# Steps of an RWKV scan moved among the levels of a block inverse, and two exponentials split

## The reference, cut to what matters

```python
# decay, keys and rates, for each direction d (1 runs backwards)
w_raw = heads(w0[d] + jnp.tanh(xw @ w1[d]) @ w2[d])
decay = jnp.exp(-jnp.exp(-jax.nn.softplus(-w_raw) - 0.5))
a = jax.nn.sigmoid(heads(a0[d] + (xa @ a1[d]) @ a2[d]))
k_d = kh * (1 + (a - 1) * k_a_h)
...
def step(S, inp):
    w_t, k_t, v_t, kk_t, kka_t = inp[:5]
    S = (S * w_t[:, :, None, :]
         - jnp.einsum('bhij,bhj->bhi', S, kk_t)[..., None] * kka_t[:, :, None, :]
         + v_t[..., None] * k_t[:, :, None, :])
    y = jnp.einsum('bhij,bhj->bhi', S, inp[5]) if emit else None
    return S, y
```

## Time and profile before

| | us |
|---|---|
| median of 3 runs | 4827.68 (4825.2 to 4829.55) |
| the profiled execution | 4823.43 |
| its span, first to last instruction | 4821.6 |
| PE busy in the span | 4601.2 (95%) |
| DVE busy | 2700.9 (56%) |
| ACT busy | 1047.4 (22%) |
| the rounds of the scan, from 1434.9 to 2171.0 | 736.1 |

### The profile page before, as it was taken

The page is one execution under the profiler, slowest core; times in us unless marked ns, Lnnn a source line. Parts: engine busy times, 40 slices in busy tenths (PEclk is TensorE's granted clock), DMA queues, the critical chain, the costliest instruction groups (busy, mean ns, idle before and its releaser), DMA issues.

```text
span 4821.6 us, 70246 instructions
## 1 busy us (share of the span) xinstructions
PE 4601.2 (95%) x29914; PEld 3255.1 (68%) x29914; DVE 2700.9 (56%) x4820; ACT 1047.4 (22%) x2337; POOL 81.2 (2%) x81
## 2 busy tenths in 40 slices
PE   8999999998999899899999999989999999989998
PEld 5556555555546666665887788645887788645886
DVE  3172445535336776653555766674656766674656
ACT  1052100002016666642001110152001010151000
POOL 0000000000000000000000000020000000020000
PEclk9998999998999999998999999989999999989999
DMA  5211122221200000012222222211222122211221
GB/s 237 105 45 53 54 105 108 116 79 46 83 0 3 3 3 3 3 38 96 88 88 88 73 79 78 97 53 53 88 88 96 70 88 79 88 53 70 88 88 44
DMA packets 27046, 339.09 MB, mean 70 GB/s; under 512 B 3024, under 2 KB 3024, under 8 KB 6896
## 3 DMA queue, kind: packets, MB, share of 16 engines
q1 hardware_dynamic: 24048, 324.51, 17.9%
q0 software_dynamic: 2688, 10.09, 0.6%
HBM read 330.40 MB, written 4.19 MB: 69 GB/s over the span
## 4 chain that ended last, share of the span: by engine, by line
PE 88%; DVE 7%; ACT 4%; issue 2%; DMA 0%; SPq 0%; ACTq 0%; DVEq 0%
PE ps L1363 45%; PE ps L1081 23%; PE ps L1562 2%; PE ps L1153 2%; PE ps L1534 1%; PE ps L1493 1%; PE ps L1545 1%; PE ps L1610 1%; PE ps L1123 1%; ACT arena L1803 1%; PE ps L1304 1%; PE ps L1618 1%; PE ps L1431 1%; PE ps L1483 1%; DVE arena L2293 1%
## 5 line engine op out<-in xcount | busy, mean ns | idle before, releaser
L1363 PE MATMUL ps<-arena 128*128 128x256 f32 (+1 forms) x9096 | 2112.7, 395 | 15.1 <-DVE arena L2629 15.1
L1363 PEld LDWEIGHTS ps<-arena 128*128 128x128 f32 x9096 | 1735.9, 191 | 379.6 <-DVE arena L2629 17.5
L1081 PE MATMUL ps<-arena 128*128 128x512 f32 (+3 forms) x3104 | 1153.4, 533 | 10.7 <-ACT arena L1754 7.4
L1081 PEld LDWEIGHTS ps<-arena 128*128 128x128 f32 x3104 | 585.6, 192 | 566.4 <-issue 401.2
L2620 DVE TENSOR_TENSOR arena<-ps,arena 128x512 f32<-128x512 f32 (+1 forms) x250 | 157.6, 630 | 316.1 <-PE ps L1363 314.3
L2620 DVE TENSOR_TENSOR square<-ps,square 128x512 f32<-128x512 f32 (+1 forms) x145 | 99.1, 683 | 175.9 <-PE ps L1363 175.9
L2561 DVE TENSOR_TENSOR arena<-arena 128x1024 f32<-128x1024 f32 (+2 forms) x153 | 190.5, 1245 | 8.7 <-ACT arena L1754 5.4
L1944 ACT COPY square<-ps 128x512 f32<-128x512 f32 (+1 forms) x65 | 37.2, 573 | 659.3 <-PE ps L1363 591.9
L1562 PE MATMUL ps<-arena 64*64 64x64 f32 x3072 | 133.6, 230 | 19.9 <-ACT arena L2017 19.2
L2881 DVE COPY_PREDICATED arena<-const,ps 128x256 f32<-128x256 int32 x192 | 85.3, 445 | 114.2 <-PE ps L1562 111.0
L1944 ACT COPY arena<-ps 128x384 f32<-128x384 f32 (+1 forms) x35 | 18.5, 529 | 575.1 <-PE ps L1363 549.2
(11 more groups left out here) (341 smaller groups left out, 4868.4 us busy)
## 6 DMA issues: line engine op xcount, KB each, us to landing
arena<-in_panels SPq DMA_DIRECT2D x144, 2048.0 KB, 7.7
arena<-in_panels SPq DMA_DIRECT2D x9, 1536.0 KB, 6.4
arena<-in_bias POOLq DMA_DIRECT2D x8, 512.0 KB, 4.5
arena<-in_x_in SPq DMA_DIRECT2D x1, 3072.0 KB, 10.6
x_save<-arena POOLq DMA_DIRECT2D x1, 2048.0 KB, 7.5
arena<-x_save POOLq DMA_DIRECT2D x1, 2048.0 KB, 12.8
out_x<-arena SPq DMA_DIRECT2D x8, 256.0 KB, 2.2
arena<-in_panels SPq DMA_DIRECT2D x1, 1792.0 KB, 11.6
```

The lines of the kernel that those rows point to most:

```text
L1081: ins = pe.matmul(dest, left(k), right(k), start=(k == 0), stop=(k == nk - 1))
L1363: ins = pe.matmul(bank[:, j * cut.side:(j + 1) * cut.side], left[:, k, j * P:(j + 1) * P], right[k], start=(k == 0), stop=(k == cut.rows - 1))
```

## The change

Four things move; no instruction is added or taken away.

1. Part 0 of every scanned chunk stands one step earlier (0, 4, 8, 12 in place of 1, 5, 9, 13). The first one so comes between the key products of the two directions in step 0, beside the couplings.
2. Direction 0's two exponentials stood together behind step 7 of a round of kind 1. Now the first stands behind step 8 and the second behind step 11, each behind the left copies of both directions.
3. Direction 1's two stood together behind step 2 of kind 2. The first stays, the second goes behind step 5.
4. In kind 1 `rate_k` goes from step 1 to 2 (direction 0) and from 2 to 5 (direction 1), and the key and rate of direction 0 from steps 3 and 4 to 4 and 5.

```diff
-        SCAN_AT = (1, 2, 3, 5, 6, 7, 9, 10, 11, 13, 14, 15)
+        SCAN_AT = (0, 2, 3, 4, 6, 7, 8, 10, 11, 12, 14, 15)
...
-            {0: [("run", 1, 1)], 1: [("rate_k", 0, 0)], 2: [("rate_k", 1, 0), ("run", 1, 2)], 3: [("key", 0, 0)],
-             4: [("rate", 0, 0)], 7: [("exp", 0, 0)]},
...
+            {0: [("run", 1, 1)], 2: [("rate_k", 0, 0), ("run", 1, 2)], 4: [("key", 0, 0)],
+             5: [("rate_k", 1, 0), ("rate", 0, 0)], 8: [("exp", 0, 0)], 11: [("exp", 0, 1)]},
...
                 elif what == "exp":
-                    act.wait_ge(sem("running"), 6 * p + 3 * d + 3)
-                    if 2 * p + d > 0:
-                        act.wait_ge(sem("decayed"), 2 * p + d)
-                    act.activation(f_inc, f_inv[d], ACT.Exp, scale=-E_HALF).then_inc(sem("exponents"), one("exponents"))
-                    act.activation(f_inv[d], f_inv[d], ACT.Exp, scale=E_HALF).then_inc(sem("exponents"), one("exponents"))
+                    if i == 0:
+                        act.wait_ge(sem("running"), 6 * p + 3 * d + 3)
+                        if 2 * p + d > 0:
+                            act.wait_ge(sem("decayed"), 2 * p + d)
+                        act.activation(f_inc, f_inv[d], ACT.Exp, scale=-E_HALF).then_inc(sem("exponents"), one("exponents"))
+                    else:
+                        act.activation(f_inv[d], f_inv[d], ACT.Exp, scale=E_HALF).then_inc(sem("exponents"), one("exponents"))
```

More of the change, by code:

```diff
@@ L723, in build_program @@
              12: [("run", 0, 1)], 13: [("lora", 0, 1), ("run", 0, 2)], 14: [("lora", 1, 1), ("run", 1, 0)]},
-            {0: [("run", 1, 1)], 1: [("rate_k", 0, 0)], 2: [("rate_k", 1, 0), ("run", 1, 2)], 3: [("key", 0, 0)],
-             4: [("rate", 0, 0)], 7: [("exp", 0, 0)]},
[1 row of a table removed]
+            {0: [("run", 1, 1)], 2: [("rate_k", 0, 0), ("run", 1, 2)], 4: [("key", 0, 0)],
+             5: [("rate_k", 1, 0), ("rate", 0, 0)], 8: [("exp", 0, 0)], 11: [("exp", 0, 1)]},
+            {0: [("kr", 0, 0)], 1: [("kr", 0, 1), ("kr", 0, 2)], 2: [("exp", 1, 0)], 3: [("key", 1, 0)], 4: [("rate", 1, 0)], 5: [("exp", 1, 1)],
              6: [("kr", 1, 0)], 7: [("kr", 1, 1), ("kr", 1, 2)], 8: [("k_sum", 0, 0)], 9: [("bk", 0, 0)], 10: [("bk", 0, 1)],
@@ L731, in build_program @@
         EARLY += [("recip", 0, i) for i in range(RECIPS)] + [("rate_k", 0, 0), ("rate_k", 1, 0), ("kk", 0, 0)]
-        EARLY += [("run", d, i) for d in range(2) for i in range(3)] + [("exp", 0, 0)]
+        EARLY += [("run", d, i) for d in range(2) for i in range(3)] + [("exp", 0, 0), ("exp", 0, 1)]
         EARLY += [(what, d, 0) for d in range(2) for what in ("key", "rate")] + [("k_sum", 0, 0)]
-        LATE = [("kr", 0, 0), ("kr", 0, 1), ("kr", 0, 2), ("bk", 0, 0), ("bk", 0, 1), ("exp", 1, 0), ("kr", 1, 0), ("kr", 1, 1),
+        LATE = [("kr", 0, 0), ("kr", 0, 1), ("kr", 0, 2), ("bk", 0, 0), ("bk", 0, 1), ("exp", 1, 0), ("exp", 1, 1), ("kr", 1, 0), ("kr", 1, 1),
                 ("kr", 1, 2), ("bk", 1, 0), ("bk", 1, 1), ("bonus", 0, 0)]
```

## The result

The changed kernel takes 4790.99 us (median of 4 runs, 4786.77 to 4795.97) against 4826.44 for the kernel before on the same chip: 0.993 of it, with a 95% interval of 0.9917 to 0.9942. That is 35 us faster. I had forecast 4816 and a range that ended at 4805: the direction is right, the size is three times mine. In the profiled executions the span falls from 4821.6 to 4789.8 us, 31.8 us; the rounds of the scan, counted from the first key product to the end of the last output product, shrink by 30.0 of them, from 736.4 to 706.4 us.

A forecast was written before the change was run, and what follows sets the result against it. PE bounds the kernel (busy 95%), with about 60 us open in the scan's rounds. -22+4.6+3.2+2.1+2.1-2.5+0.5-0.9+1 = -11.9 from 4823.43 gives 4811.5; the median runs 4.25 above the profiled run: forecast 4816, range 4805 to 4828.

The forecast's parts named there:

- The exponentials: Direction 0's exponentials behind the left copies, kind 1: steps 8 to 11 save 21 to 24 us over seven rounds, taken as 22.
- The working through round 22: Same steps without exponentials, 5.71 us against 8.66 in round 10: the first exponential hides completely behind the left copies there.
- the 5.2 us: Expected length of steps 8 to 11 in kind 1 at the full clock, with ACT 0.7 us late for step 10.
- The clock: Kind 1, step 0: the new 1.6 us wait brings one more fall to 0.50, +1 us, from -6 to +6.
- more is left: Rival: the clock stays at 1.00 behind step 8 and at step 0; -20 us, 4808, chance 0.18.
- the wait only moves: Rival: ACT is behind in steps 10 and 11, the clock falls after both waits every round; 4823, chance 0.26.
- -11.9: The sum of all the prediction's terms in us, taken from the profiled 4823.43 us.
- Part 0 at step 0, kind 1: The wait for the zeroing stays, 1.6 us; loss 0.5 us in seven rounds, 1.1 in round 22, together 4.6.
- Kind 2: Part 0's move costs rounds of kind 2 0.4 us at step 0 (eight rounds, 3.2), 0.3 at step 8 (seven, 2.1).
- the +0.13: Part 0 at step 4, between the turned inverses: +0.13 us in sixteen rounds (kinds 0 and 2, and 22), 2.1 us.
- Step 9: Part 0 from step 9 to 8: step 9 0.03 us shorter, but +0.3 in seven kind 2 rounds where DVE is full.
- step 6: Kind 2: direction 1's second exponential ahead of a scan copy, 0.1 us wait instead of part 1's 0.2 for `w`: nothing.

The follow-up runs named there:

- exp_only: The kernel before with only the exponentials moved and split (steps 8 and 11 of kind 1, 2 and 5 of kind 2): 4799.7 us, 24.6 below before.
- zero_after: The changed kernel with the state set to zero earlier, in the last scanned chunk of the pair before: 4779.9 us, 11.1 below the changed kernel.
- scan_only: The kernel before with only the scan's new steps (part 0 of every chunk one step earlier): 4824.2 us against 4824.3.
- first_only: The kernel before with only part 0 of each first chunk moved from step 1 to step 0: 4826.4 us, 2.2 above before.

## Why the prediction was right in direction and wrong in size

**The exponentials: right, with luck in it.** Steps 8 to 11 of the seven rounds took 25.1 us less together; I had 22, from a span of 21 to 24. The working through round 22 was sound for the wait. But the 5.2 us took the full clock for given behind a wait of 1.4 us that stays, while round 22 fell behind the same wait. In exp_only the clock fell as it did in round 22, the steps took 5.6 to 5.8 us in six of the rounds, and the seven gained 21.4. The other 3.7 us, and the 5.06 us of round 10, came with part 0 at step 8, for which my sum had no gain of the clock.

**The clock: the step that failed.** I wrote "I take one more such fall: +1". In the trace the four falls at steps 0 to 2 are gone, 1.5 us each (round 7 went from 11.4 to 10.2 us there, though a round that had not fallen got 0.35 us longer). So are the fall of round 22 in steps 8 to 11, 1.1 us, and what reached beyond step 11 in round 16, another 1.1. That is about -8 in place of +1, without the 3.7 us above. My reason was that a longer wait is closer to a fall. The runs show that the length of the wait did not decide: 1.4 us at step 1 brought falls in three to five of eight rounds, depending on the moment, 1.5 us at step 0 in none of the rounds of seven kernels. The same holds for "Against: round 22 falls to the lower clock on the wait of 1.38 us alone, which stays": the wait stayed, and the fall went, because a product with the state now stands between the left products behind it. The rival "more is left" is what happened, and I gave it 0.18; its price, -20, was too small too. The rival "the wait only moves" has a slip in its sum: 1.2 us less saved in seven rounds and 4 more for the clock make 12.4 on top of -11.9, which is 4828 and not 4823.

**Part 0 at step 0, kind 1: right.** The wait moved and grew (12.3 us in all, 1.53 in round 10), and steps 0 to 2 take 0.35 us more where the clock had not fallen before; I had 0.5; in round 22 it is 0.94, and I had 1.1. That zero_after gives 11.1 us for this wait, 12.0 in the rounds of the traces, confirms that it is bare.

**Kind 2: too dear.** I expected some 5 us in eight rounds; it is 0.17 us in each of rounds 5 to 20 and nothing in round 2, some 1 us in all. Round 11 takes 28.8 us, and I had 29.3. The product with the state costs 0.23 us in step 0 and not 0.4, since it overlaps its neighbours. In step 4 the +0.13 came out exactly. Step 9 lost 0.19, not 0.3. And step 6 gained 0.29 us, where part 1 had waited for `w`: I had written that off against the exponential, which then did not stand in the way.

**Outside the rounds** the span is 1.8 us shorter, with the same work; the lower level lasted 144 us there behind the rounds, against 154. That is not the change's, and the other kernels scatter by as much.

Together: of the missing 20 us 9 are the clock, 3 the exponentials, 1 step 0 and 2 lie outside the rounds; the 5 that are left are for the most part kind 2. The round of kind 1 shows the sum of it: 29.2 us, where I had 31.5 to 32.

## What to carry to other kernels

A wait costs its own length and, behind it, the matmuls that run at the lower level; whether they do depends, in these kernels, on what PE has to do on both sides of it and on the moment. So price a wait from both kinds of rounds in the trace, and when the clock's share is as large as the waits themselves, give the case that it vanishes its full chance. Table loads and long activations belong directly behind the last copy that PE waits for, and no longer than PE has work. And where a wait is for something that needs no input, like a zeroing, move that and not the one who waits.

## What the runs showed of the hardware that was not expected

- TensorE's clock fell from 1.00 to 0.50 (2.4 to 1.2 GHz) behind 20 of 35 waits of 1.4 us that stood between short products and turned inverses, and behind none of 56 waits of 1.5 us between the key products (seven kernels with the first part at step 0 and the wait kept). At step 8, behind the same 1.4 us, it fell behind 12 of 14 waits, and with eight short matmuls between the two left products behind 3 of 42. The Trainium skill (page "TensorE: Matmul & The Clock Gate", section "A second HAM failure mode: psum-queue depth-cycling") tells of a bf16 kernel in which small idle gaps between groups of matmuls come so often that the clock swings between its two levels; the swing is seen here too, behind single gaps of 1.4 us.
- Equal busy shares of the steps do not tell it. Steps 0 to 2 have the same wait in rounds 10 and 16 of the kernel before, and the clock fell in one and held in the other. The wait of round 16 began 0.1 us earlier against the beat of the level's changes than that of round 10, just outside the quarter in which all 20 falls lie.
- Where the first long wait no longer brought a fall, the next one brought a longer one: 10.2 us, where it was 6.8 in most rounds, behind the exponentials in five rounds each of scan_only and first_only, and in round 16 of the kernel before. So a fall that is avoided can be paid later, and a part that saves waits may show no time until the last one goes.
